# The last down projection in two passes over its column blocks, tokens 256 to 543 first and tokens 0 to 255 after them

## The reference

```
def rmsnorm(x, g):
    r = lax.rsqrt(jnp.mean(xf * xf, axis=-1, keepdims=True) + EPS)
    return (xf * r).astype(x.dtype) * g

x = x + swiglu(rmsnorm(x, norm_ffn), w_gate, w_up, w_down)   # w_down (2816, 1024)
return rmsnorm(x, norm_final), ...                           # y_prompt (512, 1024), y_sample (32, 1024)
```

## Time and profile before

| | us |
|---|---|
| median of 3 runs (945.57, 945.96, 948.23) | 945.96 |
| the profiled execution | 944.17 |
| its span, first to last instruction | 942.4 |
| PE busy | 922.2 (98%) |
| DVE busy | 512.6 (54%) |
| ACT busy | 259.4 (28%) |
| POOL busy | 62.9 (7%) |
| DMA queue q1, share of 16 engines | 28.0% |

### The profile page before, as it was taken

The page is one execution under the profiler, slowest core; times in us unless marked ns, Lnnn a source line. Parts: engine busy times, 40 slices in busy tenths (PEclk is TensorE's granted clock), DMA queues, the critical chain, the costliest instruction groups (busy, mean ns, idle before and its releaser), DMA issues.

```text
span 942.4 us, 17750 instructions
## 1 busy us (share of the span) xinstructions
PE 922.2 (98%) x7273; PEld 917.0 (97%) x7273; DVE 512.6 (54%) x923; ACT 259.4 (28%) x378; POOL 62.9 (7%) x64
## 2 busy tenths in 40 slices
PE   6999999999998999999999999999999999999995
PEld 6999999999998999999999999999999999999995
DVE  4567777666566333355578655555533355555452
ACT  7333332223233333222211211222212122112331
POOL 0000010000004000000024200000000000000330
PEclk8999999999999999999999999999999999999998
DMA  9221232221222222222222222222223422221312
GB/s 282 94 73 63 90 96 90 86 73 64 89 89 70 72 85 88 90 89 89 89 90 90 90 90 90 89 89 67 67 84 116 134 82 80 78 65 48 90 48 95
DMA packets 90230, 83.50 MB, mean 89 GB/s; under 512 B 1612, under 2 KB 88756, under 8 KB 90196
## 3 DMA queue, kind: packets, MB, share of 16 engines
q1 hardware_dynamic: 90196, 83.03, 28.0%
HBM read 80.65 MB, written 2.38 MB: 88 GB/s over the span
## 4 chain that ended last, share of the span: by engine, by line
PE 97%; DMA 1%; issue 0%; SPq 0%; DVE 0%; ACT 0%; ACTq 0%; DVEq 0%
PE ps_main L425 32%; PE ps_main L423 31%; PE ps_main L424 31%; DMA tok<-in_x_prompt_dram 1%; PE ps_g L544 1%; PE ps_g L455 0%; PE ps_t L455 0%; PE ps_g L545 0%; PE ps_g L464 0%; PE ps_t L529 0%; PE ps_t L448 0%; SPq L325 0%; PE ps_main L630 0%; ACT tok L808 0%; ACTq L109 0%
## 5 line engine op out<-in xcount | busy, mean ns | idle before, releaser
L423 PE MATMUL ps_main<-act_hi,w_hi 128*128 128x272 f32 x2336 | 676.5, 290 | 3.2 <-DVE sig L861 3.2
L425 PE MATMUL ps_main<-act_hi,w_lo 128*128 128x272 f32 x2336 | 677.5, 290 | 0.0
L424 PE MATMUL ps_main<-act_lo,w_hi 128*128 128x272 f32 x2336 | 672.8, 288 | 0.0
L423 PEld LDWEIGHTS ps_main<-act_hi,w_hi 128*128 128x128 f32 x2336 | 440.8, 189 | 4.3 <-DVE sig L861 3.4
L424 PEld LDWEIGHTS ps_main<-act_lo,w_hi 128*128 128x128 f32 x2336 | 441.4, 189 | 0.2 <-issue 0.2
L425 PEld LDWEIGHTS ps_main<-act_hi,w_lo 128*128 128x128 f32 x2336 | 440.1, 188 | 0.0
L645 ACT CAST w_hi<-w_raw 128x2048 fp32r<-128x2048 f32 x50 | 95.3, 1906 | 283.6 <-PE ps_main L425 283.5
L848 DVE TENSOR_TENSOR w_lo<-w_raw,w_hi 128x2048 fp32r<-128x2048 f32 x50 | 128.0, 2559 | 48.2 <-ACT w_hi L645 48.0
L650 ACT ACTIVATE w_hi<-w_raw,g_cols 128x256 fp32r<-128x256 f32 x224 | 92.5, 496 | 97.8 <-PE ps_main L425 97.4
L854 DVE SCALAR_TENSOR_TENSOR w_lo<-w_raw,g_cols,w_hi 128x256 fp32r<-128x256 f32 x224 | 91.4, 480 | 47.6 <-ACT w_hi L650 47.3
L1153 DVE TENSOR_TENSOR gate_sb<-ps_main,r_all 128x544 f32<-128x544 f32 x22 | 16.0, 725 | 73.6 <-PE ps_main L425 73.3
(11 more groups left out here) (151 smaller groups left out, 364.2 us busy)
## 6 DMA issues: line engine op xcount, KB each, us to landing
w_raw<-in_w_in_dram SPq DMA_DIRECT2D x27, 1024.0 KB, 5.1
w_raw<-in_w_gate_dram SPq DMA_DIRECT2D x11, 1024.0 KB, 5.3
w_raw<-in_w_up_dram SPq DMA_DIRECT2D x11, 1024.0 KB, 5.3
w_raw<-in_w_down_dram SPq DMA_DIRECT2D x8, 768.0 KB, 4.7
w_raw<-in_w_down_dram SPq DMA_DIRECT2D x8, 640.0 KB, 4.3
w_raw<-in_w_pa_dram SPq DMA_DIRECT2D x4, 1024.0 KB, 4.9
w_raw<-in_w_pb_dram SPq DMA_DIRECT2D x4, 1024.0 KB, 5.0
w_raw<-in_w_o_dram SPq DMA_DIRECT2D x4, 1024.0 KB, 5.0
```

What stands on the lines that cost most here:

```text
L423: pe.matmul(out, whi, xhi, start=(k == 0), stop=False)
L424: pe.matmul(out, whi, xlo, start=False, stop=False)
L425: last = pe.matmul(out, wlo, xhi, start=False, stop=(k == blocks - 1))
```

## The change

`down_2` becomes two phases of eight units each. `down_2a` goes over the eight column blocks for tokens 256 to 543 (288 tokens: chunks 2, 3 and the sample), `down_2b` again over the same eight blocks for tokens 0 to 255 (chunks 0 and 1). Each unit of either phase loads and splits its weights anew and has 10 x 3 = 30 matmuls, of 288 or 256 tokens. The sums, root, scaling and stores of the first group are written into the program between units of the second phase.

```diff
+    CUT = 2 * P
+    LATE = {"down_2a": (CUT, N), "down_2b": (0, CUT)}
+    CHUNKS = {"down_2a": (2, 3, CH), "down_2b": (0, 1)}
+    ON_ACT = {"down_2a": (3,), "down_2b": (1,)}
...
             with sp.Fori(0, 4) as j:
                 for s in range(2):
-                    load_down(ph["down_2"], j, s, NF1 * P, NF2)
-            for c in range(CH + 1):
...
+                    load_down(ph["down_2a"], j, s, NF1 * P, NF2)
+            with sp.Fori(0, 4) as j:
+                for s in range(2):
+                    load_down(ph["down_2b"], j, s, NF1 * P, NF2)
+            sp.wait_ge(y_ready_act, 1)
+            store_y(3)
+            sp.wait_ge(y_ready, 2)
+            store_y(2)
+            store_y(CH)
+            sp.wait_ge(y_ready, 3)
+            store_y(0)
+            sp.wait_ge(y_ready_act, 2)
+            store_y(1)
...
+            def down(p, j, s, ready=None):
+
+                a, b = LATE[p.name]
+                out = ps_main[:, s, 0, 0:b - a]
+                pe.wait_ge(lo_ready, p.unit(j, s))
+                pair_free(p, j, s, 0)
+                for k in range(NF2):
+                    if ready is not None:
+                        ready(k)
+                    whi, wlo = w_hi[:, s, k * P:(k + 1) * P], w_lo[:, s, k * P:(k + 1) * P]
+                    xhi, xlo = act_hi[:, H0 + k, a:b], act_lo[:, H0 + k, a:b]
+                    pe.matmul(out, whi, xhi, start=(k == 0), stop=False)
+                    pe.matmul(out, whi, xlo, start=False, stop=False)
+                    last = pe.matmul(out, wlo, xhi, start=False, stop=(k == NF2 - 1))
+                last.then_inc(tile_half, 2)
...
+            down(pa, 3, 1)
+            turn_y(pa, 3, 0)
+            down(pb, 0, 0)
+            turn_y(pa, 3, 1)
+            down(pb, 0, 1)
+            sum_y(pa, 0)
+            turn_y(pb, 0, 0)
+            down(pb, 1, 0)
+            turn_y(pb, 0, 1)
...
+            def scale_y(p, norm):
+                act.wait_ge(msq_done, norm - 1)
+                act.activation(root[:], msq[:], ACT.Sqrt).then_inc(root_done, 1)
+                act.wait_ge(rstd_ready, norm - 4)
+                for c in ON_ACT[p.name]:
+                    act.activation(tok[:, c, :], tok[:, c, :], ACT.Copy, scale=rstd[:, c:c + 1]).then_inc(y_ready_act, 1)
...
+            split_hi(pb, 0, 1)
+            y_squares(pb, 0, 0, 1, first=True)
+            split_hi(pb, 1, 0)
+            y_squares(pb, 0, 1, 1, first=True)
+            scale_y(pa, 5)
...
+            def norm_y(p, part):
+                dve.wait_ge(ysums_turned, part + 1)
+                sums = ps_main[:, 0, 1, :]
+                for c in CHUNKS[p.name]:
+                    n = ROWS[c]
+                    last = dve.tensor_scalar(msq[0:n, c:c + 1], sums[0:n, c:c + 1], 1.0 / D, EPS, ALU.mult, ALU.add)
+                last.then_inc(msq_done, 1)
+                inverse_root(5 + part, last=rstd_ready, done=part + 1)
+                dve.wait_ge(y_in_tok, KD * (part + 1))
+                for c in CHUNKS[p.name]:
+                    if c not in ON_ACT[p.name]:
+                        n = ROWS[c]
+                        dve.tensor_scalar(tok[0:n, c, :], tok[0:n, c, :], rstd[0:n, c:c + 1], None,
+                                          ALU.mult).then_inc(y_ready, 1)
...
+            split_lo(pb, 1, 0)
+            take_x2(pb, 1, 0, 1)
+            norm_y(pa, 0)
+            take_y(pb, 0, 1, 1)
```

More of the change, by code:

```diff
@@ new lines, in turn_y, with sum_y @@
+            def turn_y(p, j, s):
+                pe.wait_ge(dve_out[s], p.out_before(j, s) + 2)
+                for n, c in enumerate(CHUNKS[p.name]):
+                    dst = ps_misc[s][0:P, 0, n * P:(n + 1) * P] if c < CH else ps_misc[s][0:NS, 1, 0:P]
+                    last = pe.transpose(dst, x_last[:, s, c * P:c * P + ROWS[c]], ident[:, :])
+                last.then_inc(y_turned, 1)
+            def sum_y(p, part):
+                pe.wait_ge(ysum_done, KD + part * (KD - 1))
+                pe.wait_ge(ysq_done, KD * (part + 1))
+                for c in CHUNKS[p.name]:
+                    n = ROWS[c]
+                    out = ps_main[0:n, 0, 1, c:c + 1]
+                    pe.matmul(out, y_sum[:, c * P:c * P + n], ones[:, 0:1], start=True, stop=False)
+                    last = pe.matmul(out, y_sq[:, 1, c * P:c * P + n], ones[:, 0:1], start=False, stop=True)
+                last.then_inc(ysums_turned, 1)
@@ L634, in _ @@
+            down(pb, 1, 0)
+            turn_y(pb, 0, 1)
+            with pe.Fori(1, 3) as j:
+                down(pb, j, 1)
+                turn_y(pb, j, 0)
+                down(pb, j + 1, 0)
+                turn_y(pb, j, 1)
+            down(pb, 3, 1)
+            turn_y(pb, 3, 0)
+            turn_y(pb, 3, 1)
+            sum_y(pb, 1)
         @block.scalar
@@ L823, in loop, with inverse_root @@
                 steps[0] = before + count * (j - first)
-            def inverse_root(norm, last=None):
+            def inverse_root(norm, last=None, done=1):
                 x, r, t = msq[:], rstd[:], newton[:]
@@ L837, in inverse_root @@
                     end.then_inc(last, 1)
-                    dve.wait_ge(last, 1)
+                    dve.wait_ge(last, done)
             def split_lo(p, j, s, norm=False):
@@ L1195, in _, with take_x2 @@
             steps[0] = before + NF2 // 2 * per_pass
-            p = ph["down_2"]
-            def take_x2(j, s, first=False):
+            def take_x2(p, j, s, part, first=False):
+                a, b = LATE[p.name]
                 if not first:
[L1202 to L1207, removed]
@@ L1238, in _ @@
[L1238 to L1247, removed]
+                last = dve.tensor_tensor(tok[:, cs[0]:cs[0] + 2, bass.ds(P * m, P)],
+                                         ps_misc[s][:, 0, 0:2 * P].rearrange("p (c n) -> p c n", c=2),
+                                         gf.rearrange("p (a n) -> p a n", a=1).to_broadcast((P, 2, P)), ALU.mult)
@@ new lines, in _ @@
+            dve.wait_ge(gf_loaded, 16)
+            pa, pb = ph["down_2a"], ph["down_2b"]
+            take_x2(pa, 0, 0, 0, first=True)
+            split_lo(pa, 0, 1)
+            take_x2(pa, 0, 1, 0, first=True)
+            take_y(pa, 0, 0, 0)
+            split_lo(pa, 1, 0)
+            take_x2(pa, 1, 0, 0)
+            take_y(pa, 0, 1, 0)
+            with dve.Fori(1, 3) as j:
+                split_lo(pa, j, 1)
+                take_x2(pa, j, 1, 0)
+                take_y(pa, j, 0, 0)
+                split_lo(pa, j + 1, 0)
+                take_x2(pa, j + 1, 0, 0)
+                take_y(pa, j, 1, 0)
@@ L1250, in _ @@
+            take_x2(pb, 3, 1, 1)
+            take_y(pb, 3, 0, 1)
+            take_y(pb, 3, 1, 1)
+            norm_y(pb, 1)
         @block.gpsimd
```

142 lines of the change are left out of this document (72 added, 70 removed).

## The result

The changed kernel takes 954.96 us (median of 6 runs, 952.24 to 956.81) where the kernel before takes 945.77 (6 runs, 943.72 to 948.23): a ratio of 1.0095, 95% interval 1.0078 to 1.0111. It is slower by 0.95%, and 1 us above the top of the predicted range, 954.0. Its profiled execution took 955.02, its span is 953.3.

A forecast was written before the change was run, and what follows sets the result against it. PE, busy 98% of the span, was taken as the bound. Last unit 9.12 us later less 4.4 of tail gives 4.7: 944.17 to 948.9, plus 1.8 for the median, 950.7; own range 948.5 to 952.2, full range 947.8 to 954.0.

The forecast's parts named there:

- step 1: Start of the first pass: PE waits for unit 1's low part, 0.66 us idle.
- step 2: First pass: units 1, 3, 5, 7, 9 start 8.75 apart, set by landing plus both splits; PE idle 2.04 us.
- step 3: Behind unit 9: PE does the first group's six sums, 1.45 us.
- step 4: Ahead of unit 12: the first group's mean, root and scaling delay its weight splits; PE idle 3.2 us.
- step 5: Unit 14: its load is issued only when unit 12's low part is done; PE idle 0.73 us.
- tail, given back: Behind the last product: less turning, fewer sums (1.14) and fewer stores (3.0); tail 8.6 for 13.03, 4.4 us back.
- the sign that the prediction named against itself: ACT's high parts released by PE all along, not by the DMA, would mean that step 2 falls.
- The clock's fall: Rival: PE's clock falls to half in the gap ahead of unit 12, 2.1 us more, 952.8; chance 0.22.
- Later landings: Rival: loads land later when they come twice as often; at 4.9 us the time is 953.7; chance 0.12.
- stores that stay in the tail: Rival: the first group's stores move with the last two, the 3.0 us are not saved, 953.7; chance 0.04.
- Sooner landings: Rival: loads land sooner, the raw slot's loop is 7.95, steps 2 and 5 are gone, 948.0; chance 0.13.
- The faster case: Rival: unit 12's split does not wait for the norm and the loads keep up, 944.7; chance 0.04.

The follow-up runs named there:

- the trimmed version: Changed kernel with norm behind the last weight split, all splits over 1280 columns, first group's sums in three matmuls, chunks 0 and 1 scaled and stored in halves: 941.84 us.
- splits over 1280: Changed kernel with both weight splits of the two passes over the 1280 columns that are read, not 2048: 947.91 us.
- loops written out: Changed kernel with PE's two loops over units written out, same instructions in the same order: 952.88 us, a single run.
- norm late: Changed kernel with the first group's mean, root and scaling moved behind the last weight split: 950.29 us.
- half loads: Changed kernel with each load of the two passes bringing 5 of 10 weight blocks (320 KB), for timing alone: 949.68 us.
- the two versions with short splits: Changed kernel with weight splits over 1280 columns, 947.91 us, and the same with the first group's norm behind the last weight split, 943.77 us.
- the two edits: Changed kernel with the first group's norm behind the last weight split and weight splits over 1280 columns: 943.77 us.

## Why the prediction was wrong

The direction was right, and the forecast's price of the change was 4.7, measured 9.2. By terms, for the last unit's end (predicted; in the profile):

| | predicted | measured |
|---|---|---|
| step 1, unit 1 waits for its low part | 0.66 | 0.64 |
| step 2, the raw slot's chain | 2.04 | 2.6 |
| step 3, six sums | 1.45 | 1.16 |
| step 4, the norm ahead of unit 12 | 3.2 | 3.5 |
| step 5, unit 14's load | 0.73 | 0.62 |
| turnings, unit starts, rounding (measured: the rest) | 1.04 | 1.1 |
| half clock | 0 | 3.0 |
| sum | 9.12 | 12.6 |
| tail, given back | 4.4 | 4.4 |

**The clock.** This is the step that failed: the sum left the clock at 1.00 through every gap, half clock put at 0, and only a rival had it fall, once, for 2.1, at a chance of 0.22. It fell twice, in units 9 and 12, and cost 3.0. Three things in that step were off.

- *The evidence.* Against a fall stood the 3.2 us wait of the earlier trace rows, behind which the clock stayed up. That was the outcome of one trace. PE makes this same wait, 3.49 to 3.50 us from matmul to matmul, in all eleven traces; behind it the clock was at 0.50 in nine of them, and stayed at 1.00 only in the kernel before and in the trimmed version. By these traces a fall is the likelier outcome behind a gap of this length.
- *The number of places.* The second gap, ahead of unit 9, exists only by the next error.
- *The size.* The rival took 2.8 for one fall, from the 6.8 us at half clock near the kernel's start. Here the clock was back before the unit was over, and a fall took 1.5.

With PE kept busy the kernel takes 951.64, within the forecast's own range of 948.5 to 952.2 and 0.9 over its 950.7: without the clock the sum held. (That range is itself narrower than the bounds it follows from: 944.17 + 1.8 + 7.1 is 953.1.) How long a gap must be stays open. The clock fell behind 2.18 (splits over 1280), 2.28 and 3.64 (after), 3.08 and 3.57 (loops written out), and not behind 2.02 (norm late) or 3.61 (half loads). Length alone doesn't decide, as the wait that all traces share shows best, and no run here says what else does.

**Step 2, right in size, wrong in kind.** It had the raw slot 8.75 apart for four rounds against PE's 8.24, 0.5 a round. PE's side was too short: a matmul goes by its columns. PE timeline, after, steps of 288 tokens first, then 256:

```profile
871.74 0.29 PE L630 MATMUL ps_main<-act_hi,w_hi 128*128 128x288 f32 x1
871.87 0.29 PE L631 MATMUL ps_main<-act_lo,w_hi 128*128 128x288 f32 x1
872.00 0.29 PE L632 MATMUL ps_main<-act_hi,w_lo 128*128 128x288 f32 x1
...
919.51 0.28 PE L630 MATMUL ps_main<-act_hi,w_hi 128*128 128x256 f32 x1
919.63 0.28 PE L631 MATMUL ps_main<-act_lo,w_hi 128*128 128x256 f32 x1
919.76 0.28 PE L632 MATMUL ps_main<-act_hi,w_lo 128*128 128x256 f32 x1
```

0.13 and 0.12 apart, in the mean over the units 0.133 and 0.119 without each unit's first; 272 took 0.126. Units 2 to 6 start 4.3 to 4.4 apart, two of them 8.7: level with the raw slot's chain. So the even waits didn't come and the high parts were released by PE, the sign that the prediction named against itself. In their place came two uneven ones, 0.58 ahead of unit 7 and 2.02 ahead of unit 9, from landings of 4.9 and 5.7. The bound there was 4.6, a little over the 4.1 to 4.4 of the earlier trace rows; but before, a load has 8 us, and what the latest of them does to PE isn't seen. The clock fell behind the one wait of 2 us; behind the waits of 0.2 to 1.3 us in the two passes it never did, so four of 0.5 would most likely have cost no clock. No run shows that case.

**Steps 1, 3, 4 and 5** hold within 0.3, and the norm's order was shown by moving it. With the clock fall that it brings, this one order is worth 4.1 us by the two versions with short splits; the 4.7 of the changed kernel hold unit 9's clock too, and new waits against it.

**The tail** gave 4.4 for 4.4, and the stores 3.1 of it for 3.0.

**The rivals.** The clock's fall came, twice. Later landings came, as single loads and not as a new median, which stayed at 4.3. Sooner landings and stores that stay in the tail did not. The faster case named its two conditions, a norm that no split waits for and loads that keep up; with the two edits that bring both about, the kernel takes 943.77, and the prediction had 944.7 for it.

## What to carry to other kernels

Where a change halves the work for which a weight slot is read, add up landing and splits against two such units, and take the latest landing that any trace holds, not the median: a load that had 8 us of slack never showed what its latest ones cost. On an engine that runs in order, put the norm of a finished group behind the last split that the next units wait for. And price a gap of 2 us or more in TensorE's work twice, once for its length and once for the 1.5 us that the clock may take behind it, at every place where one can arise. Look at such a gap in several traces: whether the clock falls behind it can differ from run to run, and the trace that you happen to read shows one outcome.

## What the runs showed of the hardware

- Behind the same wait of PE, 3.5 us from matmul to matmul near 292 us, the granted clock fell to 0.50 in nine traces and stayed at 1.00 in two. Each fall took 1.5 us there too: unit 1's high part starts 572.0 us after that wait in the changed kernel and 570.5 in the kernel before.
- Matmuls with a new weight block each took 0.119, 0.126 and 0.133 us for 256, 272 and 288 columns at full clock, in proportion to their columns; at half clock 272 took 0.227 and 256 took 0.213, which is the columns over 1.2 GHz. The first of a unit takes 0.1 longer behind a turning or a wait, and not behind other matmuls of its kind (0.12 behind the filling ones).
- Landings of the same 640 KB spread from 4.0 to 6.5 us. All but one of those over 5.0 had a packet of an instruction queue within them.
- POOL's add is held up while DVE's low part runs. POOL's timeline, after, beside DVE's low part and alone:

```profile
938.74 2.52 POOL L1402 TENSOR_TENSOR y_sum<-y_sum,y_sq 128x256 f32<-128x256 f32 x1 [1.27 <-ACT y_sq L829]
941.93 0.74 POOL L1402 TENSOR_TENSOR y_sum<-y_sum,y_sq 128x256 f32<-128x256 f32 x1 [0.67 <-ACT y_sq L829]
```

The same add takes 2.52 beside DVE's low part (938.38 to 940.67) and 0.74 where none runs; the low part takes 2.3 either way. It cost nothing here: the chain of waits passes through no add of POOL's.
